# Two-layer attention trunk: the last pair of each layer starts the first token tile of the output projection with seven of eight row groups, multiplies the gate projection row group by row group, and gives all remainders of w_out to VectorE

## The reference

```python
D_MODEL = 1024; SEQ = 1024; DEPTH = 2          # batch 1, float32
cond = silu(c)
for i in range(DEPTH):
    shift, scale, gate = split(cond @ w_ada[i] + b_ada[i])
    h = rms_norm(x, g_pre[i]) * (1 + scale) + shift
    u = h @ w_in[i]                              # 1024 x 4096
    mix_in, z = u[..., :3072], u[..., 3072:]
    if i % 2 == 0: y = stick_breaking_attention(mix_in)      # 16 heads of 64
    else:          y = diff_attention(mix_in, ...)           # 8 heads, two maps each, ALiBi, chunk mask
    y = (y * silu(z)) @ w_out[i]                 # the output projection, 1024 x 1024
    x = x + gate * rms_norm(y, g_post[i])
```

## Time and profile before

| what | value |
|---|---|
| median of 3 runs | 1529.79 us (1529.43 to 1530.43) |
| the profiled execution | 1529.82 us, span of the core 1528.0 us |
| PE busy | 1392.9 us, 91% of the span |
| DVE busy | 1014.4 us, 66% |
| ACT busy | 904.4 us, 59% |
| POOL busy | 381.0 us, 25% |

### The profile page before, as it was taken

How to read it: one execution, slowest core, us unless ns; L and a number is a source line. 1 busy time by engine, 2 the same in 40 slices (tenths; PEclk the granted TensorE clock), 3 DMA queues, 4 the chain that set the end, 5 groups by cost and what they waited for, 6 DMA issues and landing times. The chain is left out here.

```text
span 1528.0 us, 23331 instructions
## 1 busy us (share of the span) xinstructions
PE 1392.9 (91%) x7206; PEld 1145.5 (75%) x7206; DVE 1014.4 (66%) x1801; ACT 904.4 (59%) x1758; POOL 381.0 (25%) x274
## 2 busy tenths in 40 slices
PE   6889999999999999868896999999999999995898
PEld 3578787878888787756775788787887878783776
DVE  4557878787878787978268565656565655657415
ACT  3556666666656566663346366767676767757322
POOL 2012323232222232333032213222221222112214
PEclk8989999999999999978997999999999999996999
DMA  9011111111111111221043101010000010002014
GB/s 342 34 35 56 56 56 56 55 55 55 55 55 55 53 57 48 92 81 35 3 150 110 42 28 29 27 41 27 27 27 27 27 41 27 27 16 109 1 67 168
DMA packets 88590, 89.88 MB, mean 59 GB/s; under 512 B 3065, under 2 KB 68834, under 8 KB 88546
## 3 DMA queue, kind: packets, MB, share of 16 engines
q1 hardware_dynamic: 88256, 89.15, 18.4%
q10 hardware_dynamic: 290, 0.18, 0.1%
HBM read 80.92 MB, written 8.40 MB: 58 GB/s over the span
## 5 line engine op out<-in xcount | busy, mean ns | idle before, releaser
L713 PE MATMUL bank<-h_hi,w_hi 128*128 128x512 f32 x976 | 398.7, 409 | 12.9 <-POOL w_lo L683 4.9
L713 PE MATMUL bank<-h_hi,w_lo 128*128 128x512 f32 x976 | 393.9, 404 | 0.0
L713 PE MATMUL bank<-h_lo,w_hi 128*128 128x512 f32 x976 | 391.6, 401 | 0.0
L1475 POOL TENSOR_TENSOR sa<-sa,keep 128x128 f32<-128x128 f32 (+7 forms) x128 | 172.1, 1347 | 460.3 <-DVE keep L1341 460.3
L713 PEld LDWEIGHTS bank<-h_hi,w_hi 128*128 128x128 f32 x976 | 186.6, 191 | 45.7 <-issue 14.3
L713 PEld LDWEIGHTS bank<-h_hi,w_lo 128*128 128x128 f32 x976 | 186.0, 191 | 34.6
L713 PEld LDWEIGHTS bank<-h_lo,w_hi 128*128 128x128 f32 x976 | 186.4, 191 | 31.0
L1341 DVE TENSOR_TENSOR_SCAN keep<-keep 128x128 f32<-128x128 f32 (+7 forms) x128 | 175.5, 1371 | 20.0 <-ACT keep L1234 18.8
L683 POOL TENSOR_TENSOR w_lo<-w_raw,w_hi 128x1024 fp32r<-128x1024 f32 x31 | 74.0, 2386 | 322.4 <-ACT w_hi L677 322.4
L1233 ACT ACTIVATE sa<-bank 128x512 f32<-128x512 f32 (+2 forms) x192 | 94.3, 491 | 81.3 <-PE bank L1121 38.4
L1246 ACT ACTIVATE wt_hi<-bank 128x512 fp32r<-128x512 f32 (+2 forms) x192 | 87.7, 491 | 64.2 <-PE bank L1137 60.0
(11 more groups left out here) (221 smaller groups left out, 2972.3 us busy)
## 6 DMA issues: line engine op xcount, KB each, us to landing
w_raw<-in_w_in_dram SPq DMA_DIRECT2D x63, 512.0 KB, 4.0
ada_slice<-in_w_ada_dram SPq DMA_DIRECT2D x64, 256.0 KB, 2.7
p_ada<-in_w_ada_dram SPq DMA_DIRECT2D x8, 1024.0 KB, 13.3
wo_raw<-in_w_out_dram SPq DMA_DIRECT2D x8, 1024.0 KB, 5.2
p_x<-in_x_dram SPq DMA_DIRECT2D x8, 512.0 KB, 8.5
o_x<-in_x_dram SPq DMA_DIRECT2D x8, 512.0 KB, 4.1
x_between<-o_res SPq DMA_DIRECT2D x8, 512.0 KB, 2.9
o_x<-x_between SPq DMA_DIRECT2D x8, 512.0 KB, 4.1
```

Source lines behind the costliest of these rows:

```text
L713: mm = nc.tensor.matmul(self.bank[half][:, :], w[:, k, :], h[:, k, half * HALF:(half + 1) * HALF], start=(i == 0), stop=(i == GROUP - 1))
L1475: nc.gpsimd.tensor_tensor(a[:, at:S], a[:, at:S], m["keep"][KEEP[t]][:, at + 1:S + 1], ALU.mult).then_inc(weighted, 1)
```

## The change

In the last pair of both layers:

- Token tile 0 is split in two pieces. `early_split_hi` and `early_split_lo` do seven row groups at step `EARLY_AT` (4 in layer 0, 3 in layer 1); the eighth follows at the old kind of place. The 48 matmuls of tile 0 become a first stretch `EARLY` of 42 (both h with `wo_hi`, 28, and then both with `wo_lo`, 14) that needs nothing of the last pair, and a rest of 6.
- `MULTIPLY` of layer 0 was 0 up to step 8 and then 17 or 18 a step. It is now 7 in each of steps 5 to 8, 14 in step 9, 15 in each of steps 10 to 19. Layer 1 had 48 in each of steps 7 to 10; it has 10, 16, 16 in steps 4, 5, 6 and 30, 40, 40, 40 in steps 7 to 10. `halves` cuts a step's share in two, at the end of tile 0 where that falls inside it.
- Layer 1 multiplies z row group by row group (as layer 0 did), so three of the four loads of w_out can be issued during steps 0 and 1 instead of after them; both halves of z are then copied at step 1. `wo_hi` is made in steps 1 to 4 (before: 4 to 6).
- All eight `wo_lo` go to DVE, two a step: steps 5 to 8 in layer 0 (one on each engine in the same steps before) and 2 to 5 in layer 1 (before: 4 to 6, shared with POOL).
- In layer 0 the tile order `LAST` has both wide groups of head 0 before those of head 1; the packing of head 1 on DVE moves from steps 0 and 1 to steps 1 and 2; the sums of w_ada from steps 4 to 11 to steps 7 to 14; the gates from step 16 to 18; the splits of tiles 0, 1, 2, 3 from steps 8, 9, 13, 16 to 10, 10, 12, 14.

```diff
+    def early_split_hi(self, act, pack):
+        act.wait_ge(pack.lo_done, done(4 * PAIRS - 1))
+        ks = slice(0, KT - 1)
+        self.nc.scalar.activation(self.y_hi[0][:, ks, :], self.m["y"][:, ks, self.tokens(0)],
+                                  ACT.Copy).then_inc(self.early_hi, 1)
...
+    def early_split_lo(self, dve):
+        dve.wait_ge(self.early_hi, self.layer + 1)
+        ks = slice(0, KT - 1)
+        self.nc.vector.tensor_tensor(self.y_lo[0][:, ks, :], self.m["y"][:, ks, self.tokens(0)],
+                                     self.y_hi[0][:, ks, :].bitcast(F32), ALU.subtract).then_inc(self.early_lo, 1)
...
+            if n < self.EARLY:
+                lo = n >= 4 * L
+                t, (h, i) = 0, divmod(n - 4 * L if lo else n, L if lo else 2 * L)
+                k, part = (i, 1) if lo else (i // 2, (0, 2)[i % 2])
+                begin, end = n in (0, 2 * L), False
+                if n < 2 * L and i % 2 == 0:
+                    pe.wait_ge(self.weights_hi_done, KT * self.layer + k + 1)
+                if n == 4 * L:
+                    pe.wait_ge(self.weights_lo_done, KT * self.layer + KT)
+                if begin:
+                    pe.wait_ge(self.early_lo, self.layer + 1)
+                    pe.wait_ge(proj.sz_done, done(2 * (PAIRS - 1) + h))
+            elif n < 2 * GROUP:
+                t, (h, part) = 0, divmod(n - self.EARLY, MULS)
+                k, begin, end = L, False, part == MULS - 1
+                if n == self.EARLY:
+                    pe.wait_ge(self.weights_hi_done, KT * self.layer + KT)
+                    pe.wait_ge(self.lo_done, self.splits(0))
+            else:
...
+                if begin:
+                    if h == 0:
+                        pe.wait_ge(self.lo_done, self.splits(t))
                     pe.wait_ge(self.kept, 2 * (AHEAD * self.layer + t - 1) + h + 1)
...
+def halves(f, l):
+    c = 2 * GROUP if f < 2 * GROUP < l else (f + l) // 2
+    return (f, c), (c, l)
...
-    LAST = Order([(0, 3), (1, 3), (0, 2), (1, 2), (0, 1), (1, 1), (0, 0), (1, 0)])
+    LAST = Order([(0, 3), (0, 2), (1, 3), (1, 2), (0, 1), (1, 1), (0, 0), (1, 0)])
...
-    LAST_ADA_AT = {s: k for k, s in enumerate(range(4, 12))}
+    LAST_ADA_AT = {s: k for k, s in enumerate(range(7, 15))}
+    LAST_LO_AT = {1: 2, 2: 3}
+    EARLY_AT = 4
-    MULTIPLY = shares(AHEAD * 2 * GROUP, [0] * 9 + [1] * (STEPS - 9))
...
+    MULTIPLY = (shares(OutProjection.EARLY, [0] * 5 + [3, 3, 3, 3, 6]) +
+                [(f + OutProjection.EARLY, l + OutProjection.EARLY) for f, l in
+                 shares(AHEAD * 2 * GROUP - OutProjection.EARLY, [1] * (STEPS - 10))])
+    AHEAD_AT = [{10: (0, 1), 12: (2,), 14: (3,), STEPS - 1: (AHEAD,)}.get(s, ()) for s in range(STEPS)]
...
-            sp.wait_ge(proj.group_done, done(8 * PAIRS - 1))
-            outp.load_weights(sp, w_out)
+            outp.load_weights(sp, w_out, lambda n: (z_freed, n + 1) if n + 1 < KT // 2
+                              else (proj.group_done, done(8 * PAIRS - 1)))
...
+    OUT_HI_AT = {1 + k // 2: (k, k + 1) for k in range(0, KT, 2)}
+    OUT_LO_AT = {2 + k // 2: (k, k + 1) for k in range(0, KT, 2)}
+    EARLY_AT = 3
-    MULTIPLY = shares(AHEAD * 2 * GROUP, [0] * 7 + [1] * (STEPS - 7))
+    MULTIPLY = (shares(OutProjection.EARLY, [0] * 4 + [5, 8, 8]) +
+                [(f + OutProjection.EARLY, l + OutProjection.EARLY) for f, l in
+                 shares(AHEAD * 2 * GROUP - OutProjection.EARLY, [3, 4, 4, 4])])
```

More of the change, by code:

```diff
@@ L884, in multiply @@
+    EARLY = 2 * MULS * (KT - 1)
     def multiply(self, pe, first, last, proj):
+        L = KT - 1
         for n in range(first, last):
[L887 to L894, removed]
@@ L1178, in share @@
                     proj.multiply(pe, p, 6 * GROUP + f, 6 * GROUP + l, freed=z_freed)
-                    outp.multiply(pe, *cut(*MULTIPLY[s]), proj)
+                    outp.multiply(pe, *halves(*MULTIPLY[s])[part], proj)
                     return
@@ L1437, in pair @@
                         z_gate(p, half)
-                    if not first and s in LO_OWN:
-                        pack.lo(dve, p, LO_OWN[s])
+                    lo_own = LO_OWN if project else LAST_LO_AT
+                    if not first and s in lo_own:
+                        pack.lo(dve, p, lo_own[s])
                     if project and s in LO_NEXT:
@@ L1481, in pair @@
                         weigh(p, s)
-                    for k in () if project else OUT_LO_AT.get(s, ()):
-                        if k % 2:
-                            outp.weights_lo(pool, k)
             proj.split_lo(pool, 0, 3)
@@ L1770, in pair @@
                         outp.keep(act, t, h)
-                    for k in () if project else range(*OUT[s]):
+                    for k in () if project else OUT_HI_AT.get(s, ()):
                         outp.weights_hi(act, k)
+                    if s == EARLY_AT and not project:
+                        act.wait_ge(y_done, done(NG * p - 1))
+                        outp.early_split_hi(act, pack)
                 inverse_root(p, NG - 1)
@@ L1904, in pair @@
                         combine(p, s - 1)
-                    for half in Z_AT[s]:
+                    for half in (Z_AT if project else LAST_Z_AT)[s]:
                         keep_z(p, half)
@@ L1916, in pair @@
                                 pack.lo(dve, p + 1, n)
-                    for k in () if project else range(*OUT[s]):
-                        if k % 2 == 0:
-                            outp.weights_lo(dve, k)
+                    for k in () if project else OUT_LO_AT.get(s, ()):
+                        outp.weights_lo(dve, k)
+                    if s == EARLY_AT and not project:
+                        outp.early_split_lo(dve)
             for n in range(4):
```

59 lines of the change are left out of this document (34 added, 25 removed).

## The result

The changed kernel took **1519.6 us** (median of 4 runs, 1518.5 to 1520.6), the one before 1529.6 (4 runs, 1528.8 to 1530.4): ratio 0.9936, 95% interval 0.9923 to 0.9948. It is 10 us faster; 1521.4 was predicted, the range was 1512 to 1527. The profiled execution took 1520.6 us.

What follows compares the result with a forecast made beforehand. PE, busy 91% of the span, bounds the kernel; its holes ahead of the saturated stretches are DVE's. 1529.8 - 2.4 (layer 0) - 6.0 (layer 1) = 1521.4 us, range 1512 to 1527.

Steps and rivals of the forecast that it cites:

- this part of the sum is firm: Both layers: matmuls moved wholly into PE's holes save 0.231 us each, 6.5 us in layer 0 and 9.7 in layer 1.
- rival (c): Early matmuls stand in PE's list ahead of scores and values that DVE and ACT need: +4 us, 1534; chance 0.07.
- Layer 0, when it begins: Walk along DVE: last `wo_lo` done at 699.7, so step 9's output matmuls begin at 700, as before (700.32).
- next late is the early remainder itself: Layer 0, ahead of step 5's `o_part`: DVE's early remainder ends about 671 and three PE matmuls wait for it.
- New waits in step 10: Layer 0: PE waits 1.9 us for the eighth row group and 1.4 us for ACT's copy of tile 0.
- wait for the parked copy: Layer 1, step 7: tile 1's 24 matmuls wait 4 us for ACT's copy of tile 0, done about 1424.5.
- DVE's walk: Layer 1: +6.4 us up to step 4, then -0.8, -0.5, -5.6 for steps 4 to 6; step 7 begins at 1418.3.
- Of 5.9 us removed, 1.3 are left: Layer 0: with the hole at step 2 gone, step 5's `o_part` comes at 674.9 instead of 676.21.
- 0.7 us a step: Layer 0: contention of `wo_lo` with POOL's `weigh`, in place of 0.35, would make layer 0 -1.0 and the whole 1522.8.
- (b): Rival: the holes take everything and waits for ACT's copy are short; layer 0 -8, layer 1 -10, 1512; chance 0.27.
- (d): Rival: the gains are eaten, within the noise, by what the waits cost; 1527 to 1532; chance 0.11.
- DVE waiting on scores in steps 4 to 6 (then (c)): Layer 1: a sign that would show the forecast wrong and point to the slower rival, 1534, chance 0.07.

Runs made afterwards that it cites:

- e4: The changed kernel with no output matmuls ahead of step 9 in layer 0 and step 7 in layer 1; 1513.4 us, ratio 0.9891.
- e5: The changed kernel without early output matmuls in layer 0 only, layer 1 keeping its 42; 1511.5 us, ratio 0.9881.
- e9: e7 with ACT's copy of tile 0 moved ahead of its exponentials (layer 1) and its copy to `o_part` (layer 0); 1499.1 us, ratio 0.9793.
- e7: The changed kernel with layer 0's 28 early hi matmuls in steps 6 to 8 and its lo ones behind step 9's values; 1509.1 us, ratio 0.9867.
- e12: e9 with no early matmuls in step 4 of layer 1, 20 in step 5 and 22 in step 6; 1499.9 us, ratio 0.9800.
- e10: e7 with the old row tile order and packing of layer 0's last pair; 1511.3 us, ratio 0.9875.
- e11: The kernel before the change with only every remainder of w_out put on DVE, in the old steps; 1522.7 us, ratio 0.9950.

## Why the prediction was right, and where it was not

The total (1521.4 against 1519.6) came out right, with layer 0 at -2.4 against -0.35 measured and layer 1 at -6.0 against -7.86. That the sum fits better than either layer is luck: one error is 2.0 us, the other 1.9 the other way.

**The step that failed: "this part of the sum is firm".** 28 x 0.231 = 6.5 us and 42 x 0.231 = 9.7 us were booked as gains, and the rest as smaller corrections. Taken out alone, the early matmuls of layer 0 turn out to cost 8.5 us and those of layer 1 to gain nothing in C (e4, e5). The price per matmul is right; that a matmul which goes into a hole has no other effects is not. PE takes its list in order, and an output matmul that waits for DVE closes the list for values and scores that DVE itself waits for. The prediction had this as rival (c) at 0.07, but priced it by the matmuls' length (12 and 14 us for all of them at the low clock) and not by their waits: in step 9 seven matmuls stand ahead of the values, and DVE waits 6.35 us. Its count of 34 for layer 1 is also short: there are 42 in steps 4 to 6. In layer 1 C is 91.5 with none early and 85.2 with the early ones and a prompt copy of tile 0 (e9). A kernel with a prompt copy and none early wasn't run, so how much of this the early matmuls bring is open.

**Layer 0, when it begins.** As a number the walk was good. Shifted by the 1.29 us between the two starts of A, the early remainder ended at 669.4 (predicted 671), the o_part of step 5 came at 674.3 (674.9), the last remainder ended at 699.0 (699.7) and the output matmuls of step 9 began at 699.06 (700). The contention, 1.4 us for the eight remainders, was 11.07 - 8 x 1.175 = 1.7. But the walk read the start as DVE's limit. It was the limit of the seven lo matmuls; the values behind them began 47.3 us after the start of A in e4 (693.17), against 56.4 here (700.93). The wait at the early remainder, which the walk saw ("next late is the early remainder itself"), is the other place of the same kind, 3.9 us by e7.

**New waits in step 10.** 1.9 and 1.4 us predicted, 2.06 and 1.12 measured.

**The missing term: the clock.** Behind the holes the granted clock fell to 0.50 and 0.53, and the stretch of layer 0 lost some 3.7 us by it. The prediction used a low clock at the start only, as it was before. The sum as measured is -6.5 (28 matmuls) + 3.7 (clock) + 0.5 (values, as predicted) + 3.2 (waits) - 1.3 (the stretch began sooner: 53.24 us after the start of A, before 54.50) = -0.4; of the prediction's 0.3 for the hand-over nothing was found.

**Layer 1.** The wait for the parked copy was 3.30 us (4 predicted), at its place. Shifted by the 2.37 us between the two starts of C it ended at 1422.06 and not at 1424.5, and these 2.4 us cover the 1.9 between -6.0 and -7.86. The terms that were mis-sized lie in DVE's walk. Shifted in the same way, DVE began step 4 5.2 us later than before (predicted 6.4), spent 1.4 us less on step 5 (0.5) and 6.4 less on step 6 (5.6), and so began step 7 at 1415.7 and not at 1418.3. Waits of DVE for the second map's scores did appear (2.15 us at 1390.97), and by e12 the one in step 4 costs nothing that can be measured.

**The order of the last pair.** "Of 5.9 us removed, 1.3 are left" was in the walk: at the `o_part` of step 5 the changed kernel was 1.9 us ahead. e10, built on e7, puts the value of the order between 1.2 and 4.85, and its interval doesn't exclude none.

**Remainders on VectorE.** The saving was in the walk (3.7 us of DVE's time in layer 0, and parts of steps 4 to 6 in layer 1), and e11, which has nothing else, gains 7.2 us. The Trainium skill, GPSIMD Engine Reference, section "1. Specifications", says that GpSimd and VectorE share SBUF interfaces and that there is contention with DVE instructions that have two SBUF inputs. The rows agree: 1.17 us alone, 2.5 to 3.4 beside POOL's `wo_lo`, 1.8 each in the first pair, which began beside POOL's `weigh`. The prediction used the rule to doubt the change (0.7 us a step, 2.8 in all); the rows show 1.7. Its reason for 0.35, that most of `weigh` lies beside the lo parts, didn't hold in step 5: there `weigh` ran to 678.17 and the pair had begun at 676.79. The pair then ended 2.21 us after `weigh`, two remainders' time.

**The rivals.** (b), in which the holes take everything, gave 1512: e4 and e5 are there, but with no early matmuls in layer 0, where (b) wants them. (d) didn't occur. Of what would show it wrong, "DVE waiting on scores in steps 4 to 6 (then (c))" was seen in layer 1 and in the form of `o_part` in layer 0, beside a faster kernel. So (c)'s mechanism was at work while its total was wrong. Such a sign tells which mechanism is there, but not whether the whole is faster or slower.

## What to carry to other kernels

On an engine that takes its list in order, work put into a hole is free only if all that it waits for is ready when its turn comes. Look at what stands behind it and who waits for that: the hole's owner is often the engine that is then starved. Here 28 early matmuls whose inputs were ready gained 3.5 us, and 14 that waited, half of them ahead of values, lost 8.1. Where PE waits for a copy that frees an accumulator, try that copy ahead of ACT's other work in the step (e9: 8.2 us in A and C for tile 0's copies in the two layers, 10 in the medians). An elementwise step shared by DVE and POOL should be timed on DVE alone first: eight remainders took 9.4 us alone, and four of them 8.9 beside POOL's four.

The best kernels are e9 and e12, 1499.1 and 1499.9 us: 2.0% under the kernel before (the intervals of both ratios reach across 0.98), 1.3% under the changed one.

## Not expected of the hardware

- Two holes of nearly equal length, 2.30 us (e7, at 1391.52) and 2.32 us (e9, at 1390.92), in the same code: the six matmuls behind took 2.93 us in the one, with a grant of 0.67 over 1390 to 1394, and 1.66 in the other, at 1.00. Such a hole doesn't always bring the clock down, and why it differed here stays open. In the 10 us that end where the hole begins, PE was busy for 8.89 at a grant of 1.00 in e7 and for 9.67 at 0.95 in e9.
- DVE's remainders and splits beside POOL ended 1.07 to 1.09 us after POOL's instruction, in each of the four rows above. They were held back until its end and not merely slowed. The same is seen beside `weigh`: in the changed kernel the pair at 682.62 ended at 685.40, 2.22 us after the `weigh` that ended at 683.18.
